# Who issues the weight loads of the first projections: ScalarE in place of SyncE

## The chip, the cores and the metric

The kernel runs on one core of a Trainium2 chip. The metric is the device time of one execution in microseconds (us). TensorE (PE) multiplies, VectorE (DVE), ScalarE (ACT) and GpSimd (POOL) work on tiles in SBUF, and SyncE (SP) only issues transfers. Each of SP, ACT and POOL has a DMA queue of its own; 16 DMA engines move the data of all of them. The engines run side by side and wait for each other on semaphores. An instruction that issues a transfer is held on its engine behind the waits that stand before it.

## The reference, cut to what matters

One step of a decoder layer over a prompt of 512 rows and 8 sequences of 8 new rows (64 "sample" rows), with D = 1024. The part that the change touches is the modulation and the combined input projection:

```
mod = (silu(c) @ w_ada + b_ada).reshape(B, 6, 1, D_MODEL)      # w_ada is 1024 x 6144
shift1, scale1, gate1, shift2, scale2, gate2 = [mod[:, i] for i in range(6)]
h = x * (1 + scale1) + shift1
proj = h @ w_in                                                # w_in is 1024 x 3072
qa, ka, va, qb, kb, vb = split(proj)                           # six sections of 512
qa, ka, qb, kb get rotary positions
...
oa, win_state = attend_a(qa, ka, va)     # windows over a cache of 2048 rows
ob = attend_b(qb, kb, vb)                # pages of a cache of 2048 rows
mixed = concat(oa, ob) @ w_o ; layer norm ; ConvFFN ; layer norm
```

Among the outputs are the updated window caches: for each of the 8 sequences 2040 rows of the old keys and 2040 of the old values, moved up by 8 rows, and the new rows behind them.

## The kernel before, in words

**Weights.** A weight is loaded in chunks of 1024 x 512 floats (2 MB) into slots of the tile `ring`. `CHUNKS` lists them; chunks 0 to 3 are the first four pieces of w_ada and chunks 4 to 9 the six sections of w_in (`("in", 0)` to `("in", 5)`). From chunk 4 on, two slots alternate (`SLOT_OF`), so section c can be loaded only when section c - 2 is used up. TensorE says so by the semaphore `w_used`, after the last unit of a section. The matmuls are done in parts of float32r: VectorE and GpSimd split a section into a high part and a rest (`split_in`, and the job "split" of GpSimd, L774), and each product is three matmuls (`product`, L1723 to L1725); for the sample rows two (`sample_product`, L1718 and L1719).

**Units.** `units` are the 30 pairs (section s, tile t), s from 0 to 5 and t from 0 to 4, where t = 4 (`TP`) is the sample tile. Unit n is section n // 5, tile n % 5. Sections 0, 1, 3 and 4 are queries and keys; their results go through VectorE's rotation (L1232 to L1236), GpSimd's addition (L788) and a transposition on TensorE (L1783). Sections 2 and 5 are values; ScalarE evicts them (L910). ScalarE also evicts the transposed queries (L916). The result of a unit lies in one of four PSUM banks, so TensorE waits for the eviction of unit n - 4 before unit n.

**The late modulation.** The other eight pieces of w_ada (4 to 11) are needed only after the attention, but their products are done here, in between. Piece ch is multiplied just before unit `LATE_UNIT[ch]` (L1666; units 3, 6, 10, 13, 16, 20, 23 and 26), and summed one unit later (L1679). All of them use one buffer, `late`, so piece ch + 1 can be loaded only when product ch is done (`ada_mm`).

**Copies.** `COPY_UNIT` puts eight copies of a window cache from DRAM to DRAM (4080 KB each, `move_window`, L586) at the units 1, 4, 8, 11, 14, 18, 21 and 24. The other eight come much later. Counted in the order of issue, they are called the first to the eighth copy.

**Order of the issues.** SyncE issues all of these. It walks over the 30 units in a written order. At each unit of keys or values it first waits for the result (`rope_ok` or `pj_a`) and stores it (L604, L608, L619, L622); at the last tile of a section it loads section s + 2 (`load_chunk(6 + s)`, L544), behind the wait for `w_used` (L542); at the units of `LATE_UNIT` it loads the next late piece (`load_late`, L582), behind the wait for `ada_mm` (L580); then comes the copy of this unit. At units of queries there is nothing to store and so no wait of that kind. ScalarE has in this stage a written list of jobs too, sorted by a number: the evictions "v" at n and "q" at n + 2.5. After the projections the attention over the caches begins, for which SyncE and GpSimd load 100 MB, and SyncE starts with it behind its last store.

Of the kernel before, what the change touches and what calls it, by code (L numbers as in the profile page):

```python
# [5 lines left out]
P = 128  # L6
# [10 lines left out]
TP = SEQ // P  # L17
# [11 lines left out]
CH = 512  # L29
# [14 lines left out]
SLOT_OF = [0, 1, 2, 3] + [0, 1] * 3 + [i % 2 for i in range(19)]  # L44
CHUNK_AT = {c: i for i, c in enumerate(CHUNKS)}
# [7 lines left out]
def chunk_before(n):  # L53

    return max((i for i in range(n) if SLOT_OF[i] == SLOT_OF[n]), default=None)
# [7 lines left out]
LATE_UNIT = {4: 3, 5: 6, 6: 10, 7: 13, 8: 16, 9: 20, 10: 23, 11: 26}  # L63
# [15 lines left out]
def build(nc, a, o, spill):  # L79
# [6 lines left out]
    with ctx:  # L86
# [3 lines left out]
        def sem(name):  # L90
            return ctx.enter_context(nc.semaphore(name))
# [4 lines left out]
        def bk(i):  # L96

            return wide[i // 2][:, 512 * (i % 2):512 * (i % 2) + 512]
# [37 lines left out]
        def slot(i, t=ring):  # L136
            return t[:, i * SLOT:(i + 1) * SLOT].rearrange("p (k n) -> p k n", k=KT_D)

        def part(t, at, n):
            return t[:, at:at + n]  # L140
# [19 lines left out]
        late = part(room, 12288, KT_D * CH).rearrange("p (k n) -> p k n", k=KT_D)  # L160
# [106 lines left out]
        w_in_slot = [sem(f"w_loaded_{i}") for i in range(N_SLOTS)]  # L267
        w_used = sem("w_used")
# [9 lines left out]
        ada_mm = sem("ada_product")  # L278
# [13 lines left out]
        late_in = sem("late_modulation_loaded")  # L292
# [103 lines left out]
        units = [(s, t) for s in range(6) for t in range(TP + 1)]  # L396
# [22 lines left out]
        for r, n in enumerate(rope_units):  # L419
            sec, t = units[n]  # L420
# [56 lines left out]
        def page_numbers(eng, b, g):  # L477

            at = N_PAGES * b + 4 * g
            _, numbers = nc.values_load_multi_w_load_instructions(pages[0:1, at:at + 4], engines=[eng.engine],  # L480
                                                                  min_val=0, max_val=a["cache_k"].shape[1] - 1)
            return numbers
# [36 lines left out]
                        .then_inc(landed, 16)  # L519


        @block.sync
        def _(sp):
            def load_chunk(n):
                kind, i = CHUNKS[n]
                if (prev := chunk_before(n)) is not None and CHUNKS[prev][0] == "down":
                    half, kg = divmod(CHUNKS[prev][1], 3)
                    sp.wait_ge(g_used, FT * half + min(FT, 8 * kg + 8))
                elif prev is not None:
                    sp.wait_ge(w_used, prev + 1)  # L530
                s = w_in_slot[SLOT_OF[n]]
                dst = slot(SLOT_OF[n])
                src = a[{"ada": "w_ada", "in": "w_in", "o": "w_o", "up": "w_up", "down": "w_down"}[kind]][0]
                src = src.rearrange("(k p) n -> p k n", p=P)
                if kind == "up":
                    for g in range(2):
                        sp.dma_start(dst[:, :, 256 * g:256 * g + 256],
                                     src[:, :, DFF * g + 256 * i:DFF * g + 256 * i + 256]).then_inc(s, 16)
                elif kind == "down":
                    half, kg = divmod(i, 3)  # L540
                    nk = min(8, FT - 8 * kg)
                    sp.dma_start(dst[:, 0:nk, :], src[:, 8 * kg:8 * kg + nk, CH * half:CH * half + CH]).then_inc(s, 16)  # L542
                else:
                    sp.dma_start(dst, src[:, :, CH * i:CH * i + CH]).then_inc(s, 16)  # L544
# [29 lines left out]
            sp.dma_start(pages[:, :], a["page_table"].rearrange("b n -> (b n)").rearrange("(o n) -> o n", o=1)).then_inc(page_in, 16)  # L574


            def load_late(ch):

                if ch > 4:
                    sp.wait_ge(ada_mm, ch)  # L580
                src = a["w_ada"][0].rearrange("(k p) n -> p k n", p=P)
                sp.dma_start(late, src[:, :, CH * ch:CH * ch + CH]).then_inc(late_in, 16)  # L582

            def move_window(i, names=(("cache_win_k", "wks"), ("cache_win_v", "wvs"))):
                for name, dst in names:
                    sp.dma_start(o[dst][0, i, 0:PAST - DS], a[name][0, i, DS:PAST]).then_inc(copied, 16)  # L586


            def flat(ap):
                return ap.rearrange("t h d -> t (h d)")  # L590

            load_late(4)
            n_rope = n_v = 0
            for n, (s, t) in enumerate(units):
                kb_rows = slice(P * t, P * t + P)
                if s in (0, 3):
                    n_rope += 1
                elif s in (1, 4):
                    m = s // 3
                    sp.wait_ge(rope_ok, n_rope + 1)  # L600
                    if t < TP:
                        st = n_rope % 4
                        dst = flat((o["wkp"] if m == 0 else o["kkp"])[0, 0])[kb_rows, :]
                        sp.dma_start(dst, stage[:, st, :]).then_inc(stg[st], 16)  # L604
                    else:
                        if m == 0:
                            for b in range(DB):
                                sp.dma_start(flat(o["wks"][0, b])[PAST - DS:PAST, :],  # L608
                                             k_s[DS * b:DS * b + DS, 0, :]).then_inc(out_sem, 16)
                        else:  # L610
                            sp.dma_start(o["kks"][0].rearrange("b s h d -> (b s) (h d)"), k_s[:, 1, :]).then_inc(out_sem, 16)
                    n_rope += 1
                else:
                    m = s // 3
                    n_v += 1
                    sp.wait_ge(pj_a, n_v)
                    if t < TP:
                        dst = flat((o["wvp"] if m == 0 else o["kvp"])[0, 0])[kb_rows, :]
                        sp.dma_start(dst, vp[:, t, m, :]).then_inc(out_sem, 16)  # L619
                    elif m == 0:  # L620
                        for b in range(DB):
                            sp.dma_start(flat(o["wvs"][0, b])[PAST - DS:PAST, :],  # L622
                                         v_s[DS * b:DS * b + DS, 0, :]).then_inc(out_sem, 16)
                    else:
                        sp.dma_start(o["kvs"][0].rearrange("b s h d -> (b s) (h d)"), v_s[:, 1, :]).then_inc(out_sem, 16)
                if t == TP:
                    if s < 4:
                        load_chunk(6 + s)
                for ch, at in LATE_UNIT.items():
                    if at == n and ch < 11:  # L630
                        load_late(ch + 1)
                if n in COPY_UNIT:
                    i, which = COPY_UNIT[n]
                    move_window(i, (("cache_win_k", "wks") if which == "k" else ("cache_win_v", "wvs"),))
# [222 lines left out]
        def _(act):  # L857
# [40 lines left out]
            jobs = []  # L898
            for n, (s, t) in enumerate(units):
                if n in v_units:  # L900
                    jobs.append((n, "v", n))
                if n in tr_units and s in (0, 3) and t < TP:
                    jobs.append((n + 2.5, "q", n))
            for _, what, n in sorted(jobs):
                s, t = units[n]
                rows = P if t < TP else NS
                if what == "v":
                    act.wait_ge(pj_mm, n + 1)
                    dst = vp[:, t, s // 3, :] if t < TP else v_s[:, s // 3, :]
                    nc.scalar.activation(dst, bk(n % 4)[0:rows, :], ACT.Copy).then_inc(pj_a, 1)  # L910
                else:
                    k = tr_units.index(n)
                    act.wait_ge(qk_t, k + 1)
                    src = bk(4 + k % 2).rearrange("p (f t) -> p f t", f=4)
                    m0 = 4 * (s // 3)
                    nc.scalar.activation(qt[:, m0:m0 + 4, P * t:P * t + P], src, ACT.Copy).then_inc(qk_a, 1)  # L916
# [167 lines left out]
        def _(dve):  # L1084
# [120 lines left out]
            jobs += [(n + 0.55, "late_sum", ch) for ch, n in LATE_UNIT.items()]  # L1205
            dve.wait_ge(rope_in, 16)
            for _, what, n in sorted(jobs):
                if what == "late_rows":
                    ada_rows(n)
# [1004 lines left out]
```

## Time and profile before

| what | us |
|---|---|
| median of 3 runs | 1175.63 (1174.1 to 1181.54) |
| the profiled execution, its own time | 1176.66 |
| its span in the profile | 1175.0 |
| TensorE busy | 1023.7 (87% of the span) |
| VectorE busy | 827.1 (70%) |
| GpSimd busy | 450.5 (38%) |
| ScalarE busy | 270.8 (23%) |
| queue of SyncE (and ScalarE) | 54.2% of 16 DMA engines |

Times in the rows are counted from the start of the span. A busy share is an average over stages with different limits, so for this change the stretch of the projections counts, from 58 to 269 us, and in it what TensorE waits for. TensorE's granted clock is shown as a share of full speed: 1.00 is 2.4 GHz, and 0.50 is 1.2 GHz.

### The profile page before, as it was taken

Reading aid. Unit: us, or ns where it says so; the run is one execution under the profiler, and the core shown is the slowest. Engines: PE = TensorE matmul, PEld = TensorE weight load, DVE = VectorE, ACT = ScalarE, POOL = GpSimd, SP = SyncE. Lnnn points to the kernel's source line nnn. Section 1 sums busy time; section 2 is a strip of 40 time slices with the busy share of each in tenths; the row PEclk is TensorE's granted clock in tenths of the full one; section 3 lists DMA queues with packets and bytes.
Section 4 is the critical chain, followed back from the end, with each engine's and each line's share of the span. In section 5 each row is a group of like instructions: output and inputs, shape, how many; then the busy total and the mean of one; then the engine's idle time right before and its main releaser. Section 6 shows DMA issues by size and latency. Waiting matters only on the chain.

```text
span 1175.0 us, 23900 instructions
## 1 busy us (share of the span) xinstructions
PE 1023.7 (87%) x9297; PEld 832.1 (71%) x9297; DVE 827.1 (70%) x1545; ACT 270.8 (23%) x600; POOL 450.5 (38%) x575
## 2 busy tenths in 40 slices
PE   4599989995788888888888969999999999998994
PEld 2377657673566666566676759999999999776873
DVE  1637545644886877888876784676676767999978
ACT  0300000001343433343352032323232323000001
POOL 0423223214243444434406034565566656333323
PEclk8699999998898989898998988999999999999998
DMA  8948799978899999999963151677676622414102
GB/s 299 410 157 312 269 351 365 318 246 266 289 365 368 327 337 368 349 331 331 337 253 127 42 190 47 219 255 277 248 253 250 215 73 75 155 60 147 53 2 80
DMA packets 101030, 276.54 MB, mean 235 GB/s; under 512 B 9608, under 2 KB 33174, under 8 KB 97317
## 3 DMA queue, kind: packets, MB, share of 16 engines
q1 hardware_dynamic: 85701, 223.56, 54.2%
q0 software_dynamic: 15168, 51.39, 12.6%
q8 instruction: 74, 1.21, 0.4%
q14 instruction: 39, 0.32, 0.1%
q10 hardware_dynamic: 48, 0.05, 0.0%
HBM read 264.60 MB, written 76.69 MB: 290 GB/s over the span
## 4 chain that ended last, share of the span: by engine, by line
PE 53%; DVE 16%; issue 15%; DMA 6%; POOL 5%; SPq 2%; POOLq 2%; ACT 1%; ACTq 0%; DVEq 0%; PEldq 0%
PE wide L1723 15%; PE wide L1724 14%; PE wide L1725 14%; DMA ring<-in_w_ada 2%; DVE ring_r L1180 2%; POOLq L480 1%; PE wide L1666 1%; POOL room L509 1%; DVE ht_r L1533 1%; DMA room<-in_w_ada 1%; DVE ring L1260 1%; POOL x_sb L509 1%; POOL x_sb L805 1%; PE wide L1807 1%; DVE ring_r L1179 1%
## 5 line engine op out<-in xcount | busy, mean ns | idle before, releaser
L828 POOL TENSOR_TENSOR ring_r<-ring,ring_r 128x1024 fp32r<-128x1024 f32 x70 | 180.8, 2592 | 232.3 <-DVE ring_r L1139 201.1
L1723 PE MATMUL wide<-x_sb_r,ring_r 128*128 128x288 f32 x704 | 211.1, 300 | 11.4 <-DVE ht_r L1162 8.4
L1724 PE MATMUL wide<-ht_r,ring_r 128*128 128x288 f32 x704 | 209.3, 297 | 0.0
L1725 PE MATMUL wide<-x_sb_r,ring_r 128*128 128x288 f32 x704 | 208.7, 297 | 0.0
L1723 PEld LDWEIGHTS wide<-x_sb_r,ring_r 128*128 128x128 f32 x704 | 133.4, 190 | 14.3 <-issue 14.3
L1260 DVE STREAM_TRANSPOSE ring<-ring 128x512 f32<-128x512 f32 x208 | 129.0, 677 | 12.0 <-DMA ring<-in_cache_k 10.3
L1725 PEld LDWEIGHTS wide<-x_sb_r,ring_r 128*128 128x128 f32 x704 | 134.2, 191 | 0.0
L1724 PEld LDWEIGHTS wide<-ht_r,ring_r 128*128 128x128 f32 x704 | 133.8, 190 | 0.0
L1723 PE MATMUL wide<-ring_r,x_sb_r 128*128 128x512 f32 (+1 forms) x208 | 87.0, 418 | 11.9 <-DVE ht_r L1162 8.7
L1725 PE MATMUL wide<-ring_r,ht_r 128*128 128x512 f32 x216 | 87.2, 404 | 0.0
L1724 PE MATMUL wide<-ring_r,x_sb_r 128*128 128x512 f32 (+1 forms) x208 | 83.7, 402 | 0.0
L1548 DVE SCALAR_TENSOR_TENSOR room<-room,vec_t 128x512 f32<-128x512 f32 x44 | 55.4, 1260 | 40.0 <-ACT room L1056 40.0
L1048 ACT ACTIVATE room<-wide,vec_t 128x576 f32<-128x576 f32 x44 | 32.8, 744 | 207.1 <-PE wide L1725 202.3
L1725 PE MATMUL wide<-ring_r,room_r 128*128 128x512 f32 x192 | 77.5, 404 | 0.0
L1550 DVE SCALAR_TENSOR_TENSOR room<-room,vec_t 128x512 f32<-128x512 f32 x44 | 73.5, 1671 | 1.6
L774 POOL TENSOR_TENSOR ring_r<-ring,ring_r 128x512 fp32r<-128x512 f32 x24 | 33.5, 1401 | 88.1 <-ACT ring_r L876 44.1
L1139 DVE CAST ring_r<-ring 128x1024 fp32r<-128x1024 f32 x62 | 41.9, 687 | 34.0 <-DMA ring<-in_w_up 32.1
L1807 PE MATMUL wide<-room 128*128 128x128 f32 x320 | 53.9, 303 | 12.0 <-ACT room L950 8.6
L1723 PEld LDWEIGHTS wide<-ring_r,x_sb_r 128*128 128x128 f32 (+1 forms) x208 | 39.9, 192 | 32.6 <-issue 16.7
L517 POOL DMA_DIRECT2D x_sb<-in_cache_v x60 | 33.0, 550 | 72.5 <-issue 71.4
L1723 PE MATMUL wide<-ring_r,ht_r 128*128 128x512 f32 x136 | 55.8, 410 | 5.0 <-DVE room L1574 2.9
L1807 PEld LDWEIGHTS wide<-room 128*128 128x128 f32 x320 | 44.1, 205 | 22.1 <-ACT room L950 12.8
(271 smaller groups left out, 2119.4 us busy)
## 6 DMA issues: line engine op xcount, KB each, us to landing
ring<-in_cache_k SPq DMA_DIRECT2D x128, 256.0 KB
out_wks<-in_cache_win_k SPq DMA_DIRECT2D x8, 4080.0 KB, 19.5
out_wvs<-in_cache_win_v SPq DMA_DIRECT2D x8, 4080.0 KB, 19.3
ring<-in_w_up SPq DMA_DIRECT2D x22, 1024.0 KB, 7.6
room<-in_w_ada SPq DMA_DIRECT2D x8, 2048.0 KB, 9.7
ring<-in_cache_win_k SPq DMA_DIRECT2D x16, 1024.0 KB
x_sb<-in_cache_v POOLq DMA_DIRECT2D x60, 256.0 KB, 5.4
room<-in_cache_v POOLq DMA_DIRECT2D x56, 256.0 KB, 5.3
```

Source lines behind the costliest of these rows:

```text
L517: eng.dma_start(home[t:P:4, :, :], flat_v[1][bass.ds(pg, 1)].rearrange("a (i m) h d -> m (a i) (h d)", i=4))\
L774: nc.gpsimd.tensor_tensor(rest, w, high.bitcast(F32), ALU.subtract).then_inc(win_pool, 1)
L828: nc.gpsimd.tensor_tensor(rest, w, high.bitcast(F32), ALU.subtract).then_inc(wl_rest, 1)
L1048: nc.scalar.activation(u_b[:, k % 2, 2:2 + NT].rearrange("p (h t) -> p h t", h=2), pair, ACT.Identity, bias=vec_t[:, 0, 48 + f:49 + f]).th ...
L1139: nc.vector.tensor_copy(pair_of(n, slice(k, k + 2))[0], slot(SLOT_OF[n])[:, k:k + 2, :]).then_inc(wl_high, 1)
L1260: last = nc.vector.transpose(ktg[:, G % NK, :, 32 * t:32 * t + 32], kraw[G % NK][:, t, :].rearrange("p (g d) -> p g d", d=32))
L1548: then(nc.vector.scalar_tensor_tensor(out=c_p, in0=u_b[:, k % 2, 1:1 + SEQ], scalar=tap(1), in1=c_p, op0=ALU.mult, op1=ALU.add))
L1550: nc.vector.scalar_tensor_tensor(out=c_p, in0=u_b[:, k % 2, 0:SEQ], scalar=tap(0), in1=c_p, op0=ALU.mult, op1=ALU.add)
L1723: nc.tensor.matmul(out, left[0], right[0], start=first, stop=False)
L1724: nc.tensor.matmul(out, left[0], right[1], start=False, stop=False)
L1725: return nc.tensor.matmul(out, left[1], right[0], start=False, stop=last)
L1807: last = nc.tensor.matmul(bank[:, 0:P], pt_b[:, u % 2, P * kb:P * kb + P], vp[:, kb, m, P * (n // 2):P * (n // 2) + P], start=(kb == 0), s ...
```

## The change

The seven loads of the late pieces 5 to 11 and the four loads of the sections 2 to 5 leave SyncE's list and come into ScalarE's list of jobs. A late load has the number of its unit plus 0.3, a section the number of the sample tile's unit plus 0.4, so that each stands behind the eviction of values of the same unit and ahead of the evictions with larger numbers. The waits before them are the same ones (`ada_mm` and `w_used`), now on ScalarE. The load of piece 4, the first sections and all stores and copies stay on SyncE.

```
+        def load_late(eng, ch):
+            if ch > 4:
+                eng.wait_ge(ada_mm, ch)
+            src = a["w_ada"][0].rearrange("(k p) n -> p k n", p=P)
+            eng.dma_start(late, src[:, :, CH * ch:CH * ch + CH]).then_inc(late_in, 16)
...
-            load_late(4)
+            load_late(sp, 4)
...
-                if t == TP:
-                    if s < 4:
-                        load_chunk(6 + s)
-                for ch, at in LATE_UNIT.items():
-                    if at == n and ch < 11:
-                        load_late(ch + 1)
                 if n in COPY_UNIT:
...
+            jobs += [(at + 0.3, "late", ch + 1) for ch, at in LATE_UNIT.items() if ch < 11]
+            jobs += [(n + 0.4, "w_in", 2 + s) for n, (s, t) in enumerate(units) if t == TP and s < 4]
+            src_in = a["w_in"][0].rearrange("(k p) n -> p k n", p=P)
             for _, what, n in sorted(jobs):
+                if what == "late":
+                    load_late(act, n)
+                    continue
+                if what == "w_in":
+                    c = CHUNK_AT[("in", n)]
+                    act.wait_ge(w_used, chunk_before(c) + 1)
+                    act.dma_start(slot(SLOT_OF[c]), src_in[:, :, CH * n:CH * n + CH]).then_inc(w_in_slot[SLOT_OF[c]], 16)
+                    continue
```

## Rows read from the trace of the kernel before

**Rows 1.** Stretches: from:to, length, busy us (count) of each engine, PEclk, DMA share, GB/s.

```profile
151.00:157.00 6.00, 6.00 (x29) 3.03 (x22) 0.69 (x1) 0.00 (x0) 0.00 (x0) 0.72 0.97 340
58.00:269.00 211.00, 197.80 (x946) 143.46 (x946) 109.98 (x190) 10.37 (x18) 53.66 (x40) 0.97 0.81 285
300.00:590.00 290.00, 246.64 (x4589) 179.87 (x4589) 232.12 (x660) 107.50 (x349) 113.86 (x234) 0.93 0.97 340
```

**Rows 2.** Waits of PE, 55 to 275: us in total, times, longest.

```profile
PE wide L1666 <- DMA room<-in_w_ada: 3.6, 1, 3.6
```

**Rows 3.** Chain of waits in order of time: start, us, what.

```profile
137.74 12.79 DMA room<-in_w_ada
...
222.56 1.83 PE wide L1666 x16
...
243.86 1.83 PE wide L1666 x16
```

**Rows 4.** Timeline of SP: start, us, what it issues.

```profile
23.38 5.25 SPq L544 DMA_DIRECT2D ring<-in_w_in  x1
...
48.48 4.21 SPq L586 DMA_DIRECT2D out_wks<-in_cache_win_k  x1
...
89.21 0.59 SPq L586 DMA_DIRECT2D out_wvs<-in_cache_win_v  x1
...
120.77 0.52 SPq L586 DMA_DIRECT2D out_wks<-in_cache_win_k  x1
...
136.67 0.41 SPq L544 DMA_DIRECT2D ring<-in_w_in  x1
...
142.54 0.52 SPq L586 DMA_DIRECT2D out_wvs<-in_cache_win_v  x1
...
169.99 0.58 SPq L586 DMA_DIRECT2D out_wks<-in_cache_win_k  x1
174.42 0.40 SPq L582 DMA_DIRECT2D room<-in_w_ada  x1
...
219.25 0.53 SPq L586 DMA_DIRECT2D out_wks<-in_cache_win_k  x1
```

**Rows 5.** Timeline of ACT, evictions of units 10 and 14: start, us, [idle before <- releaser].

```profile
130.96 0.60 ACT L910 ACTIVATE room<-wide 128x512 f32<-128x512 f32 x1 [33.08 <-PE wide L1725]
...
166.20 0.59 ACT L910 ACTIVATE ring<-wide 64x512 f32<-64x512 f32 x1 [5.77 <-PE wide L1725]
```

**Rows 6.** Timeline of PE: behind unit 9, product 7, product 9.

```profile
122.20 0.63 PE L1783 MATMUL wide<-ident,mix 128*128 128x128 f32 x4 [0.45 <-PE wide L1719]
...
150.58 3.18 PE L1666 MATMUL wide<-room,c_t 128*9 128x512 f32 x16 [3.65 <-DMA room<-in_w_ada]
...
197.48 1.90 PE L1666 MATMUL wide<-room,c_t 128*9 128x512 f32 x16
```

**Rows 7.** DMA issues of 130 to 145 and 172 to 180: count, KB, us to landing.

```profile
room<-in_w_ada SPq DMA_DIRECT2D x1, 2048.0 KB, 12.8
...
room<-in_w_ada SPq DMA_DIRECT2D x1, 2048.0 KB, 21.0
```

**Rows 8.** DMA packets of 122 to 134 (third copy) and 79 to 85 (a load).

```profile
DMA packets 69, 4.19 MB, mean 350 GB/s; under 512 B 4, under 2 KB 4, under 8 KB 4
...
DMA packets 1018, 2.06 MB, mean 344 GB/s; under 512 B 10, under 2 KB 10, under 8 KB 1018
```

**Rows 9.** DMA queues (q1 SP, q0 POOL), 341 to 346, then 346 to 351: packets, MB.

```profile
q1 hardware_dynamic: 193, 1.31, 65.0%
q0 software_dynamic: 184, 0.70, 35.0%
...
q0 software_dynamic: 216, 0.82, 52.1%
q1 hardware_dynamic: 262, 0.75, 51.1%
```

**Rows 10.** Timeline of POOL: last slice of the split of section 4.

```profile
202.35 1.41 POOL L774 TENSOR_TENSOR ring_r<-ring,ring_r 128x512 fp32r<-128x512 f32 x1 [0.97 <-DVE ring_r L1177]
```

More of the change, by code:

```diff
@@ L574, in _ @@
             sp.dma_start(pages[:, :], a["page_table"].rearrange("b n -> (b n)").rearrange("(o n) -> o n", o=1)).then_inc(page_in, 16)
[L577 to L582, printed above, removed]
             def move_window(i, names=(("cache_win_k", "wks"), ("cache_win_v", "wvs"))):
```

## The prediction

> **What bounds the kernel now.** I began with the stretches that the change touches. The thirty units of the first projections run from 58 to 269 us. There TensorE is busy for 197.80 of 211.00 us, and ScalarE for 10.37 [rows 1]. So TensorE sets the pace and leaves some 13 us, and ScalarE has room. Next I asked which of those gaps a load ends. The waits of TensorE name one, 3.6 us for a piece of the modulation's weights [rows 2]. The chain of waits shows where: the piece for product 7, issued at 137.74, is on the path for 12.79 us until the product starts [rows 3]. TensorE's own timeline puts the product at 150.58, after 3.65 us of idleness [rows 6], so the piece was wanted at 146.93. Afterwards TensorE runs slow: the granted clock is 0.72 from 151 to 157 [rows 1], which is 1.2 GHz for about 3.4 us of them, and with the time from 150.58 to 151 half of 3.8 us is lost, 1.9 us. This wait costs 3.65 + 1.9 = 5.6 us in all. After the projections the cache attention keeps the DMA engines at 0.97 [rows 1], so it takes as long as before, and what the projections gain or lose moves the end of the kernel one for one.
>
> **The moved instructions.** Eleven loads of 2 MB change queue: seven pieces (5 to 11) and four sections of w_in (2 to 5). SyncE's issues of them take about 0.4 us each [rows 4]. Eleven of those on a ScalarE that is idle for 200 of 211 us are hidden between its evictions; I cost them at nothing, and at 11 x 0.4 = 4.4 us if all fell on the path. Only a full queue would make them longer: SyncE's early issue of a section took 5.25 us with several loads ahead of it [rows 4], and ScalarE has at most two loads waiting at almost every issue. The waits that move with the loads are for products that TensorE finishes before the next eviction is due, so no eviction stands behind a late one.
>
> **When loads are issued.** Section 3 is free after unit 9, at about 122 us [rows 6]; SyncE reached it only at 136.67, behind the stores of unit 9 [rows 4]. ScalarE issues it at once: 14 us earlier. Piece 7 goes out behind ScalarE's eviction of unit 10 (130.96 plus 0.6 [rows 5]), at 131.6 in place of 137.74. Section 4 follows the eviction of unit 14 (166.20 + 0.6 [rows 5]), at 166.8; before it went out just ahead of the fifth copy. Piece 9 stays at 174.42, since its product 8 sets it. SyncE loses the blocks in front of its copies of the window caches too: the second copy goes out right after the first at 48.48, not at 89.21 [rows 4]. The DMA engines have the room, with a share of 0.81 over the projections [rows 1], and only piece 5 is wanted near it; this is free. The third (120.77), fourth (142.54) and fifth (169.99) are set by row stores and stay where they are, the fifth some 0.4 us earlier.
>
> **How loads and copies share.** Everything on SyncE's queue went in order, so a load waited for the copies ahead of it and no more. Now they stand in two queues. A copy of 4.18 MB is some 64 packets: 69 packets, 4 of them small, carry 4.19 MB in the stretch that holds the third copy, 65 KB each. A load is 2 KB a packet (1018 for 2.06 MB) [rows 8]. With 16 engines a copy is four packets on each. All 64 start after 122, 1.3 us behind the issue, and before 134; at some 3 us for a packet (16 x 65 KB at 350 GB/s) a copy takes 13.7 us. A load is 64 packets an engine, done in less than the stretch's 6 us; I take 5.3. What a load gets beside a copy is not shown by the trace. Bound it: by equal bytes it gets half; by one packet in turn it gets 2 KB against 65 KB, so it stands still until the copy has ended. The nearest rows are two queues in the attention stage. From 341 to 346 us they moved 193 and 184 packets, but 1.31 and 0.70 MB: equal packets, not equal bytes. From 346 to 351 it is 262 and 216 packets and 0.75 and 0.82 MB: nearer to equal bytes, but the engines were less full there [rows 9]. I go by the first, the fuller stretch, and take turns by the packet.
>
> The Trainium skill, "DMA: Bandwidth & Descriptors", section "Queues, rings and completion order", also has each DMA engine go round its queues at packet boundaries, but counts some 9 to 17 descriptors as one packet; no row here shows groups. If it is so, the sum is plus 3 us in place of the one below (second rival).
>
> **The sum, taking turns by the packet.** *Piece 7.* The third copy's data run from about 122 to 135.8 (issue + 1.3 us, four packets). Section 3 hardly moves until then and ends at 141; piece 7 follows. At 142.54 + 1.3 = 143.8 the fourth copy starts, with some 2.8 us of piece 7 left. It stands still for the copy's 13.7 us and lands at 160.5. Before, both came ahead of that copy, in order, and piece 7 landed after 12.8 us, at 150.5 [rows 7]. Product 7 is 9.9 us later. Its slow clock stays as it is.
>
> *Section 4 and piece 9* (in the times of before, to which the 9.9 us are added). Section 4 starts at 168.1; the fifth and sixth copies arrive from 170.9, both at once, since SyncE has no wait between units 15 and 18. About 2.5 us of it are left, and the two copies take 27 us, until 198. Section 4 lands at about 199.5 less what it got in eight turns (0.7 us), so near 198.5, and piece 9 5.3 us later, at 203.7. Before, section 4 was ahead of both copies, and piece 9 between them, landing 21.0 us after 174.42 at 195.4 [rows 7], in time for its product at 197.48 [rows 6]. Now that product starts at 203.7, 6.2 us late, and runs at the slow clock (3.18 us, as product 7 [rows 6], against 1.90), and unit 20 behind it loses another 1.1 us. The split of section 4 starts up to 5 us late as well; its last slice by GpSimd came at 202.35 [rows 10] and then comes near 208, inside unit 20, which is hidden by the wait for piece 9; without that cover it alone would cost those 5 us. Sum of this place: 6.2 + 1.3 + 1.1 = 8.6 us.
>
> *The rest.* Piece 11 now leaves at 224.4, behind product 10 [rows 3], inside the seventh copy (219.25 [rows 4]), which ends at about 234; it lands by 240, and its product is at 243.86 [rows 3]. Pieces 5, 6, 8 and 10 and sections 2 and 5 have 5 us of slack or more, or no copy beside them. These cost nothing; if one of the covers is missing, it costs at most the 5.3 us of a load.
>
> Total: 9.9 + 8.6 = 18.5 us. The profiled execution took 1176.66 us, so 1195.2; it is 1.0 us above the median of 1175.63, so I forecast **1194**. By turns of up to four load packets the result is within 3 us of it; errors of 2 us in a copy's start move each term by 2. The case's own range is 1185 to 1201.
>
> **Rivals.**
> *Shares by bytes.* Then section 3 (from 123.5) is done by 134 beside the third copy, and piece 7 by about 144, before 146.93. The wait of 5.6 us goes, and section 4 and piece 9 are both done by 193. 1176.66 - 5.6 = 1171; the late stores of SyncE no longer delay anything. For it: the second stretch of [rows 9], and that the same engines have work from either queue at any time. Against it: the first stretch. It decides from a share of about a third: below that, piece 7 is not home at 146.93.
>
> *Turns of some 16 load packets.* The load gets 1.3 us after each packet of a copy. Section 3 ends at 140.5, piece 7 with two turns of the fourth copy in it at 152.7, 2.1 us later than before; piece 9, four turns behind section 4, lands at 200 and costs 1. Plus 3: 1179, range 1174 to 1183. It is the Trainium skill's rule above, worked out with the durations of this trace. "Issuing engines are not separate DMA queues", on the same page of the Trainium skill, says as well that issuing from several engines saves only the sequencer's time; no row here shows it, and by it alone nothing would change.
>
> *Only one collision.* The fourth copy or the pair misses its load by a microsecond or two, because stores or evictions fall otherwise than I took them. Then one of 9.9 and 8.6 is left: 1185 to 1187, just within 1%.
>
> *It doesn't do what it says.* ScalarE's queue, with two loads of 2 MB standing still in it, could hold ScalarE at its third issue (section 5, near 197), as SyncE was held for 5.25 us [rows 4]. The evictions of queries behind it come late while TensorE waits for piece 9 anyway; at most 3 us more.
>
> **Chances.** By the packet with both collisions 0.45; by bytes 0.29; groups of packets 0.13; one collision 0.08, near the limit, so a third of it slower; blocked ScalarE on top 0.01, slower; something outside this list that gains over 1% 0.04. A measurement of this kernel can't tell less than about 1% from no change, so within 1% is 1164 to 1187. Slower 0.49, same 0.47, faster 0.04. The range of 8 in 10 reaches from the case by bytes, 1170, to the upper end of the likeliest, 1200.
>
> **What would show it.** In the profile after: the wait of the ada product for its piece (L1666) grows from one of 3.6 us to one near 13 and one near 6, at 147 and some 10 us past 197; landings of section 3, piece 7, section 4 and piece 9 near 19, 29, 32 and 29 us after issue, counted in that order; the second copy starts before 60 us; the attention stage is as long as before. By bytes, those landings are 10 to 20 us, and no such wait is left. If the waits are there but the attention stage is shorter, then the stage was not bound by its transfers, and my one for one is wrong.

## The result, and the profile after

The changed kernel takes 1193.16 us in the median of 4 runs (1192.59 to 1193.81), against 1177.89 for the kernel before in 4 runs of its own (1174.1 to 1181.54). The ratio is **1.0153, interval 1.0123 to 1.0182**: slower by one and a half per cent. The two medians by themselves are 15.3 us apart, a ratio of 1.0130, which lies inside the interval. The forecast was 1194.

The first two groups of before have these answers in the stretches and in the waits of TensorE after the change:

```profile
58.00:269.00 211.00, 182.18 (x868) 130.57 (x867) 109.50 (x190) 8.37 (x14) 53.53 (x40) 0.92 0.75 266
151.00:162.00 11.00, 0.00 (x0) 0.00 (x0) 0.00 (x0) 0.00 (x0) 0.00 (x0) 0.61 0.83 308
```

```profile
PE wide L1671 <- DMA room<-in_w_ada: 21.3, 2, 13.6
```

Against [rows 1], TensorE is busy 15.6 us less in the same stretch, and for 11 us from 151 on it does nothing at all while the DMA engines are busy for 83%. Against [rows 2], one wait of 3.6 us has become two, 21.3 us together. TensorE's timeline places them (product 6, product 7, product 9, product 10; L1671 is L1666 of before):

```profile
124.35 1.90 PE L1671 MATMUL wide<-room,c_t 128*9 128x512 f32 x16
...
162.14 3.60 PE L1671 MATMUL wide<-room,c_t 128*9 128x512 f32 x16 [13.60 <-DMA room<-in_w_ada]
...
217.51 3.60 PE L1671 MATMUL wide<-room,c_t 128*9 128x512 f32 x16 [7.66 <-DMA room<-in_w_ada]
...
240.34 1.90 PE L1671 MATMUL wide<-room,c_t 128*9 128x512 f32 x16
```

The issues of ScalarE and SyncE after the change, to be held against [rows 4]:

```profile
123.62 0.38 ACTq L908 DMA_DIRECT2D ring<-in_w_in  x1
...
132.56 0.38 ACTq L527 DMA_DIRECT2D room<-in_w_ada  x1
...
178.72 0.37 ACTq L908 DMA_DIRECT2D ring<-in_w_in  x1
...
186.70 0.37 ACTq L527 DMA_DIRECT2D room<-in_w_ada  x1
```

```profile
52.29 0.59 SPq L586 DMA_DIRECT2D out_wvs<-in_cache_win_v  x1
...
122.36 0.52 SPq L586 DMA_DIRECT2D out_wks<-in_cache_win_k  x1
...
144.15 0.52 SPq L586 DMA_DIRECT2D out_wvs<-in_cache_win_v  x1
...
182.14 0.52 SPq L586 DMA_DIRECT2D out_wks<-in_cache_win_k  x1
182.70 0.59 SPq L586 DMA_DIRECT2D out_wvs<-in_cache_win_v  x1
...
287.87 1.02 SPq L643 DMA_DIRECT2D ring<-in_cache_win_k  x2
```

Each issue of ScalarE takes 0.4 us and comes when the working had it: section 3 some 13 us and piece 7 some 5 us earlier than before. Section 3 leaves earlier and arrives no earlier (at 144.3 us, against 136.67 + 7.9 = 144.6 before), and piece 7 leaves earlier and arrives 11.5 us later. The four loads of ScalarE's rows above, in the same order, with the time from issue to landing:

```profile
ring<-in_w_in ACTq DMA_DIRECT2D x1, 2048.0 KB, 20.7
...
room<-in_w_ada ACTq DMA_DIRECT2D x1, 2048.0 KB, 29.5
...
ring<-in_w_in ACTq DMA_DIRECT2D x1, 2048.0 KB, 33.6
...
room<-in_w_ada ACTq DMA_DIRECT2D x1, 2048.0 KB, 30.8
```

Before, pieces 7 and 9 took 12.8 and 21.0 us [rows 7]. What happens meanwhile is in the DMA queues (packets, MB, share) from 186 to 209 us, while the fifth and the sixth copy run on SyncE's queue, q1, and section 4 and piece 9 stand in ScalarE's, q10:

```profile
DMA packets 263, 8.09 MB, mean 352 GB/s; under 512 B 23, under 2 KB 23, under 8 KB 142
## 3 DMA queue, kind: packets, MB, share of 16 engines
q1 hardware_dynamic: 136, 7.83, 97.0%
q10 hardware_dynamic: 126, 0.24, 3.8%
```

136 packets on one queue, 126 on the other; 7.83 MB against 0.24 MB. The engines are full, and the loads get a thirtieth of the bytes.

**A better yardstick than the total.** What comes after the projections took between 900 and 912 us in the executions of this study, with no tie to the variant that I can see, and the first 120 us differ by some 3 us. So for each profiled execution I also give the time from product 6 to the moment when SyncE issues its first cache load. For before this is 147.26 us, from these rows; for after 287.87 - 124.35 = 163.52, which is 16.3 us more.

```profile
122.76 1.90 PE L1666 MATMUL wide<-room,c_t 128*9 128x512 f32 x16
```

```profile
270.02 1.02 SPq L649 DMA_DIRECT2D ring<-in_cache_win_k  x2
```

| kernel | median us | ratio to before, interval | product 6 to first cache load, less 147.26 |
|---|---|---|---|
| after | 1193.16 | 1.0153 (1.0123 to 1.0182) | +16.3 |
| e1 after, copies in 2 KB packets | 1170.45 | 0.9946 (0.9923 to 0.9969) | -3.6 |
| e2 before, copies in 2 KB packets | 1176.49 | 0.9993 (0.9973 to 1.0013) | -0.1 |
| e3 only the sections moved | 1172.42 | 0.9953 (0.9932 to 0.9974) | -3.7 |
| e4 only the pieces moved | 1184.44 | 1.0071 (1.0047 to 1.0095) | +8.7 |
| e5 after, copies in 8 KB packets | 1190.38 | 1.0133 (1.0090 to 1.0176) | +13.0 |
| e6 after, four copies gated | 1175.27 | 1.0010 (0.9982 to 1.0039) | -2.0 |
| e7 after, fourth copy gated | 1184.02 | 1.0054 (1.0024 to 1.0085) | +6.1 |
| e8 after, no copies | 1168.93 | 0.9944 (0.9917 to 0.9971) | -7.0 |
| e9 after, piece 7 ahead of section 3 | 1181.28 | 1.0029 (1.0003 to 1.0055) | +4.7 |
| e10 as e9, copies at other units | 1176.29 | 0.9989 (0.9959 to 1.0018) | +0.2 |

Ratios are to runs of the kernel before on the same chip. The last column is from one execution each, and it has a noise of its own. In every kernel TensorE stands for 1.9 us ahead of the sums of product 6, between 129 and 135 us, and then runs at 1.2 GHz for a while. From 124 to 145 us the granted clock is 0.84 in e2, e3, e4 and e9, and 0.92 in before and in all others: here are before and e3.

```profile
124.00:145.00 21.00, 18.77 (x85) 14.62 (x78) 10.41 (x16) 1.20 (x2) 4.54 (x4) 0.92 0.83 279
```

```profile
124.00:145.00 21.00, 18.78 (x73) 14.93 (x73) 9.62 (x16) 1.20 (x2) 4.06 (x3) 0.84 0.99 351
```

The 0.08 of 21 us make 1.7 us, so without them these four would stand at -1.8, -5.4, +7.0 and +3.0. Why the slow stretch was longer in them isn't shown.

### The profile page after: what moved, and what is told of

Same layout as the page of the kernel before. It is cut to its first block, busy times and chain, and to the rows that moved or that the text cites. A ratio compares the mean times of both kernels' runs of the same rounds, so it can differ in the third digit from the quotient of the medians.

```text
span 1191.7 us, 23900 instructions
## 1 busy us (share of the span) xinstructions
PE 1022.1 (86%) x9297; PEld 830.3 (70%) x9297; DVE 823.1 (69%) x1545; ACT 270.8 (23%) x600; POOL 450.4 (38%) x575
## 4 chain that ended last, share of the span: by engine, by line
PE 47%; DVE 19%; issue 15%; DMA 9%; POOL 5%; POOLq 2%; SPq 1%; ACT 1%; ACTq 0%; DVEq 0%; PEldq 0%
PE wide L1728 13%; PE wide L1730 13%; PE wide L1729 13%; DMA room<-in_w_ada 5%; DMA ring<-in_w_ada 2%; DVE ht_r L1538 2%; PE wide L1671 2%; DVE ring_r L1185 2%; POOLq L480 1%; DVE ht_r L1539 1%; DVE room_r L1540 1%; POOL room L509 1%; PE wide L1868 1%; DVE x_sb L1613 1%; DVE ring_r L1144 1%
## 5 line engine op out<-in xcount | busy, mean ns | idle before, releaser
L1729 PE MATMUL wide<-ht_r,ring_r 128*128 128x288 f32 x704 | 208.9, 297 | 0.0
L1265 DVE STREAM_TRANSPOSE ring<-ring 128x512 f32<-128x512 f32 x208 | 129.0, 678 | 14.9 <-DMA ring<-in_cache_k 14.4
L1868 PE MATMUL wide<-ring,x_sb 128*32 128x128 f32 (+1 forms) x1792 | 58.8, 276 | 2.8 <-DVE ring L1265 2.7
```

What stands on the lines that cost most here:

```text
L1265: last = nc.vector.transpose(ktg[:, G % NK, :, 32 * t:32 * t + 32], kraw[G % NK][:, t, :].rearrange("p (g d) -> p g d", d=32))
L1729: nc.tensor.matmul(out, left[0], right[1], start=False, stop=False)
L1868: last = nc.tensor.matmul(bank[32 * nn:32 * nn + 32, at:at + nk], qbd[:, w % 2, g].rearrange("p i q -> p (i q)"), keys[:, g, 0:nk], start= ...
```

## The experiments

**Is it the size of the packets?** e1 changes nothing in the changed kernel but the form of the eight copies; e2 does the same to the kernel before.

```
-  sp.dma_start(o[dst][0, i, 0:PAST - DS], a[name][0, i, DS:PAST])
+  turned = lambda ap: ap.rearrange("(a b r) h d -> b a (r h d)", b=16, r=1)
+  sp.dma_start(turned(o[dst][0, i, 0:2032]), turned(a[name][0, i, DS:DS + 2032]))
+  sp.dma_start(o[dst][0, i, 2032:PAST - DS], a[name][0, i, DS + 2032:PAST])
```

> The changed kernel, but the eight window copies of the projections are written as 16 strands of 127 single rows (2 KB a packet in place of 65 KB) and a small rest. Theory 'turns' (a DMA engine serves the two queues one packet each in turn): a load now gets about half of the engines beside a copy; section 3 is in by 136, piece 7 by about 146, and both waits of the ada products (13.6 and 7.7 us in the changed kernel) shrink to under 2 us; time near 1171 to 1175, unless copies in small packets are slow themselves or hold SyncE at the issue. Rival 'queue order' (SyncE's queue goes first, whatever its packets): the waits stay near 13 and 8 us, time 1190 to 1194. Rival 'memory' (loads are slow beside any copy from DRAM to DRAM): waits stay too.

1170.45 us. The wait of 13.6 us is down to 1.7, and the one of 7.7 is gone; section 3 and piece 7 landed at 139.9 and 148.7 us, 3 to 4 us later than I had them. The rivals "queue order" and "memory" are out: the same copies stand in the same queue and move the same bytes, and only the packets are smaller. One thing more differs: SyncE is held 4 to 13 us at the issue of each small rest, so the sixth copy leaves 10 us behind the fifth and not right behind it. The third and the fourth, which make the first collision, keep their times (120.86 and 142.66).

> The kernel before with the same copies in packets of 2 KB; all loads and copies stay on SyncE's queue, in order. All theories: a load waits for the copies ahead of it as before, so nothing changes but the copies' own speed: 1174 to 1182, the wait for piece 7 still 3 to 5 us. If SyncE is held at the issue of a copy with 2032 packets, its later loads go out later, and the wait for piece 7 grows.

1176.49 us, ratio 0.9993: on one queue the size of the packets is worth nothing. The wait for piece 7 is 1.9 us, where 3 to 5 were forecast. The gain of e1 is therefore not in faster copies.

**Packets of 8 KB.** e5 is e1 with r = 4 and 1920 rows.

> The changed kernel with the eight copies in packets of 8 KB (16 strands of 30 packets, and a small rest). 'Turns, one packet each': a turn is about 0.32 us for the copy and 0.08 for the load, so some 30 of a load's 64 packets on an engine pass beside one copy. Section 3 is in near 140, piece 7 has some 16 packets left when the fourth copy comes and lands near 150.5: a wait of 3 to 4 us in place of 13.6. Piece 9 lands near its product, a wait of 0 to 1 us in place of 7.7. Time 1176 to 1178. Rival 'groups of packets' (several load packets a turn): no waits, 1171. Rival 'large and small only' (the cost hangs on something else of the strands): like the 2 KB run, 1170, or like the changed kernel, 1193.

1190.38 us, where 1176 to 1178 was forecast: the size was missed by 12 us, the law was not. The waits for pieces 7 and 9 were 11.85 and 6.91 us, in place of 3 to 4 and 0 to 1. Here are the two queues from 128 to 136 us, with a copy on q1 and a load on q10, in three kernels: after, e5 and e1.

```profile
q1 hardware_dynamic: 32, 2.09, 82.3%
q10 hardware_dynamic: 32, 0.07, 2.8%
```

```profile
q1 hardware_dynamic: 270, 2.21, 74.4%
q10 hardware_dynamic: 264, 0.54, 23.9%
```

```profile
q10 hardware_dynamic: 731, 1.50, 53.6%
q1 hardware_dynamic: 734, 1.50, 49.4%
```

Packets are one to one at 65 KB, 8 KB and 2 KB alike (32 : 32, 270 : 264, 734 : 731), and the load's share of the bytes is 3%, 20% and 50%. I had put that into numbers as if the 16 engines ran evenly. They don't. Of e5, from 152 to 158 us:

```profile
q1 hardware_dynamic: 256, 2.10, 100.0%
q10 hardware_dynamic: 37, 0.05, 2.8%
```

By turns on all engines there would be as many load packets as copy packets. There are 37 for 256, and 11 of the 37 are writes under 512 B; 16 such writes come with every load, which I take for the engines reporting their parts done. From 154 to 158 us next to nothing of the load is left:

```profile
q1 hardware_dynamic: 163, 1.34, 100.7%
q10 hardware_dynamic: 8, 0.02, 1.7%
```

Eight load packets in 4 us are one each 0.5 us, beside 163 of the copy on 16 engines, 10 for each. That fits one engine that still takes turns, while the others are done, and of the product's 11.85 us of waiting the last 5 or so were for that one. A load has landed when its last engine is done, so even a copy with a load share of 20% delays the tail of a load by most of the copy. That a slow engine is so because of the small row stores ahead is my guess; the trace doesn't name engines.

**Each part alone.** In e3 the list of ScalarE has only the jobs "w_in", and SyncE keeps the late pieces:

```
-            jobs += [(at + 0.3, "late", ch + 1) for ch, at in LATE_UNIT.items() if ch < 11]
...
+                for ch, at in LATE_UNIT.items():
+                    if at == n and ch < 11:
+                        load_late(sp, ch + 1)
```

> One part of the change alone: ScalarE issues the four sections of w_in, the late pieces stay on SyncE. 'Turns': section 3 stands still beside the third copy and ends beside piece 7 by 147; piece 7 is ahead of the fourth copy on the same queue, so its wait is under 1 us; section 4 stands still beside the fifth copy, until about 185, and is in by 188, before its split at 193.65; piece 9 goes between the fifth and sixth copy as before. No wait left: 1176.7 - 5.6 = 1171. Rival (the loss comes from section loads that start inside copies): section 4 late, 1180 or more.

1172.42 us, with no wait for a piece left. Section 3 landed 20.8 us after its issue and section 4 after 23.3 (7.9 and 8.0 before), so both did stand still beside a copy, and it cost nothing, because the splits that use them come 15 and 4 us after the landings. This version beats the kernel before by half a per cent. By the yardstick it gains 3.7 us and not the forecast 5.6; the longer slow stretch behind product 6 makes up 1.7 of the difference.

e4 is the opposite: the jobs "late" on ScalarE, `load_chunk(6 + s)` back on SyncE.

> The other part alone: ScalarE issues the late pieces 5 to 11, the sections stay on SyncE. 'Turns': piece 7 leaves at 131.6, stands still until the third copy's end at 136, then shares with section 3 and is in by about 146: no wait there, minus 5.6 us. Piece 9 leaves at 174.4 with the fifth and sixth copy in SyncE's queue, one behind the other without it, and lands only behind both, near 209 in the times of before: 12 us late and 2.4 us of slow clock. Sum 1176.7 - 5.6 + 14.4 = 1185. Rival (the sections' move makes the loss): 1171.

1184.44 us, and 8.7 us by the yardstick, where the sum had -5.6 + 14.4 = 8.8. That fit is luck: from product 6 to product 8 it gained 3.7 us, and behind product 8 it lost 12.4, each some 2 us off (1.7 of the first is the slow stretch behind product 6). Piece 9 landed 37.9 us after its issue; TensorE at product 9:

```profile
208.57 3.57 PE L1673 MATMUL wide<-room,c_t 128*9 128x512 f32 x16 [14.84 <-DMA room<-in_w_ada]
```

Here nothing but its own load stands in ScalarE's queue, and it still waits for both copies. That is the second collision by itself. Piece 7 stood only beside the rest of the third copy, landed 11.9 us after its issue and made no wait. So for the first collision both parts together are needed: section 3 ahead of piece 7 on one queue, behind the third copy, pushes it into the fourth.

**Taking copies out of the way.** e6 and e7 hold copies of the changed kernel back; e8 leaves the eight copies out, so these parts of its outputs are never written.

```
                     i, which = COPY_UNIT[n]
+                    if n in (11, 18, 21):                      # e7: if n == 11
+                        sp.wait_ge(late_in, 16 * {11: 4, 18: 6, 21: 7}[n])
+                    elif n == 14:                              # e6 only
+                        c = CHUNK_AT[("in", 4)]
+                        sp.wait_ge(w_in_slot[SLOT_OF[c]], slot_count(c))
```

> The changed kernel with one wait alone: the fourth copy waits for the landing of piece 7. This takes the first collision away and leaves the second. 'Turns': piece 7 lands near 146, so its wait of 13.6 us goes; piece 9 still lands behind two copies, 6 to 9 us late and with 2.4 us of slow clock. 1193.2 less (13.6 + 1.9 to 2.4) = 1177 to 1178. If the two waits were one effect passed on, this would come out at 1171 or at 1193.

1184.02 us, some 60% of the loss gone (+6.1 in place of +16.3). The first wait is down to 2.1 us while the second is still 5.3, so the two collisions are separate, as stated. But I forecast 1177 to 1178 and missed what the held copy hits next: it leaves at 149.10 and is in the way of piece 8, which had been free. Its product waits 4.25 us and runs slow:

```profile
173.69 3.60 PE L1673 MATMUL wide<-room,c_t 128*9 128x512 f32 x16 [4.25 <-DMA room<-in_w_ada]
```

> The changed kernel, but four of SyncE's copies wait until the load they would hit has landed: the fourth for piece 7, the fifth for section 4, the sixth for piece 9, the seventh for piece 10. Copies keep their 65 KB packets. 'Turns': piece 7 lands near 146, section 4 near 174, piece 9 near 193, no wait at any ada product; 1171, as good as the run with 2 KB packets. Rival (two queues are slower in themselves): some of the 13.6 and 7.7 us stays.

1175.27 us with a range of 1170.70 to 1185.43; by the yardstick -2.0. The big waits are gone, but four of 0.2 to 2.2 us are left (4.7 us in all). The largest is piece 7's own: with no copy beside its end it landed 18.2 us after its issue, at 149.1, and not near 146. The other three (1.55, 0.17 and 0.72 us) are for pieces 8, 10 and 11, which the held copies now delay. No gain over the kernel before is shown.

> The changed kernel with the eight copies of the projections left out (these parts of the window outputs are not written). 'Turns': no load stands beside a copy, no wait at any ada product; 1170 to 1172. The attention stage keeps its length, since no copy ran into it. If it came out well below 1170, the copies would cost more than these waits, for example in the attention stage or in the stores.

1168.93 us, 1 us under the range of the forecast, and -7.0 by the yardstick. No product waits for a piece: with no copies at all, two queues make no such wait. I take it as the floor; e1 and e3 are within 4 us of it. Of the 7.0 us, 1.6 lie between product 9 and product 10 (23.37 us here, 25.01 before), where no slow stretch follows TensorE's stop.

**Order within ScalarE's queue, and places of the copies.**

```
-  jobs += [(n + 0.4, "w_in", 2 + s) for ...
+  jobs += [(n + (0.4 if s != 1 else 1.35), "w_in", 2 + s) for ...
   e10 also:
+  COPY_UNIT = {1: ..., 4: ..., 5: ..., 8: ..., 11: ..., 14: ..., 21: ..., 24: ...}
```

> The changed kernel with one order changed on ScalarE: section 3 is loaded behind piece 7, in place of ahead of it. 'Turns': piece 7 runs from the third copy's end at 136 to about 142, before the fourth copy's first packet at 144; its wait of 13.6 us goes. Section 3 then stands still beside the fourth copy and lands near 160, just in time for its split at about 161. The second collision stays: piece 9 some 6 to 9 us late. Time 1178 to 1181. If section 3 is late too, some us more. Rival (the first wait is the price of the copy as such, whatever stands in the queue): 1193.

1181.28 us, +4.7. Piece 7 landed 12.1 us after its issue in place of 29.5, and its wait is gone, with the same copies at the same units. The number 1.35 puts the load of section 3 just behind that of piece 7. Section 3 was not caught by the fourth copy, as I had expected, but landed at 148.7 us; what is left of the loss is the second collision, a wait of 10.1 us for piece 9. So the first wait of the changed kernel was no price of the copy as such; it was a piece that missed the gap between two copies. How little it missed it by shows in the changed kernel from 148.5 to 162 us, the time of the fourth copy and of the row stores behind it: q10 moved 126 packets there, writes under 512 B among them, so at most an eighth of the 1024 of piece 7 were open when the copy came.

```profile
q1 hardware_dynamic: 244, 4.33, 83.9%
q10 hardware_dynamic: 126, 0.24, 4.7%
```

> As the run with piece 7 first, and four copies leave two units later or earlier so that no two stand behind one another beside a wanted load: the copies go out at the units 1, 4, 5, 8, 11, 14, 21 and 24 (before: 1, 4, 8, 11, 14, 18, 21, 24). 'Turns': the third runs from 102 to 116 beside piece 6, which lands near 120 against a need at 123; the sixth at 170 holds section 4 until 184, and piece 9 lands near 192, before 197.5. No wait left but for a us or two: 1171 to 1173, as the run with 2 KB packets, with copies of 65 KB. It tells whether the law is good enough to place copies by.

1176.29 us, where 1171 to 1173 was forecast; no gain is shown. (Its profiled execution, of 1184.51 us, is the slowest of its 12, with 912 us behind the projections.) No product waits for a piece any more, as planned. But the copy of unit 11 came at 142.79, 1.2 us earlier than the one at 144.01 in e9, and caught section 3 before its end: it landed 30.5 us after its issue, not 17.5, and the split waited 6.4 us for it, and TensorE 5.4 us for the slices. The law held and a plan by it isn't robust. Which load is caught hangs on a microsecond.

## Why the prediction was right, step by step

*TensorE sets the pace in the projections, and the rest passes one for one.* Right. The stage of the cache attention kept its length, as far as one execution each can tell where all lie between 900 and 912: 1175.0 - 270.02 = 905.0 us of the span are left at the first cache load before, and 1191.7 - 287.87 = 903.8 after. The DMA engines are at 0.99 in it, against 0.97 [rows 1]:

```profile
310.00:600.00 290.00, 236.67 (x4442) 173.22 (x4444) 230.63 (x654) 107.11 (x351) 112.20 (x231) 0.92 0.99 342
```

*The issues cost nothing on ScalarE.* Right, eleven of 0.4 us between evictions. ScalarE was held at an issue only in e9 and e10, where two loads were issued one right behind the other.

*The choice between bytes and packets.* Right, and now shown: one to one at three sizes. The rival "shares by bytes" and the rival "turns of some 16 load packets" are out. This kernel of before had only one fair hint, the stretch of equal packets in [rows 9]; the second stretch there spoke the other way, and I can't say why.

The rule of the Trainium skill, "DMA: Bandwidth & Descriptors", section "Queues, rings and completion order", that an engine goes round its queues at packet boundaries, agrees with the traces. The 9 to 17 descriptors that it counts to a packet do not: the turn of a load was a single record of 2 KB, by the counts above.

*The first collision, 9.9 us.* From product 6 to product 7 it was 150.58 - 122.76 = 27.82 us before and 162.14 - 124.35 = 37.79 after: 9.97 us. The collision is as told, but that it fits to a tenth is luck, for the steps inside it were off by more. I had the fourth copy start 1.3 us behind its issue. It was issued at 144.15, and from 144 to 148 us the queues moved this:

```profile
DMA packets 804, 1.63 MB, mean 408 GB/s; under 512 B 7, under 2 KB 7, under 8 KB 804
q10 hardware_dynamic: 735, 1.50, 96.7%
q1 hardware_dynamic: 69, 0.13, 8.6%
```

All 804 packets are under 8 KB, so no packet of the copy is among them; the 69 of SyncE's queue are row stores that were issued ahead of it. So the copy came 2.5 us or more later than in the working, and it found at most an eighth of piece 7 left, not half. The two errors cancel: from the copy's start to the landing of piece 7, at 162.06, it took 14 us at most, where I had 16.7 (143.8 to 160.5). At the rate of the rows above, 126 packets are 0.7 us of load. By this estimate a copy that came 0.7 us later would have met nothing, which is the rival "only one collision".

*The second, 8.6 us.* Mis-sized, with errors of opposite sign. From product 7 to product 9 it is 46.90 us before (197.48 - 150.58 [rows 6]) and 55.37 after, so product 9 came 8.5 us later, not 6.2. Most of this is a slip in my sum: 198 + 2.5 - 0.7 is 199.8 for section 4 and not 198.5, so by its own terms piece 9 lands at 205.1 and its product is 7.6 us late. Another 0.7 us is the slow clock of product 7, which I had left as it was: the product took 3.60 us in place of 3.18, and product 8 came 22.59 us behind it in place of 21.87 (172.45 - 150.58). The landings were all 1 to 2 us later than I had written (20.7, 29.5, 33.6 and 30.8 us against 19, 29, 32 and 29). And again the copy, issued at 182.14, started later than 1.3 us behind its issue: from 180.2 to 185.5 us 880 packets passed on q10, nearly all of them section 4's, and none of 65 KB on q1, whose 114 packets carried 0.12 MB.

```profile
184.73 1.90 PE L1671 MATMUL wide<-room,c_t 128*9 128x512 f32 x16
```

```profile
q10 hardware_dynamic: 880, 1.80, 93.3%
q1 hardware_dynamic: 114, 0.12, 6.3%
```

So about a seventh of section 4 was left when the two copies came, not half; it landed at 212.3 all the same, behind both, since its last engine counts.

But from product 9 to product 10 it was 25.01 us before, and 22.83 after: 2.2 us come back. Before, TensorE stood 1.9 us in that place, ahead of the sums of product 9. The trace names no releaser, but VectorE's copy of the rows of product 9 (L1125), which had its turn behind slices of the split of section 4, ended at 207.73, just ahead of them. Then TensorE ran at 0.53 of full clock from 208.9 to 212.4. After, the split began at 212.32, was well under way by the time piece 9 let TensorE go on, and neither the stop nor a slow stretch behind it is left; only product 9 itself runs slow.

```profile
207.83 1.03 PE L1679 MATMUL wide<-sum,mix 128*128 128x9 f32 x8 [1.93 <-issue]
...
222.49 1.91 PE L1666 MATMUL wide<-room,c_t 128*9 128x512 f32 x16
```

```profile
212.32 0.43 DVE L1182 CAST ring_r<-ring 128x512 fp32r<-128x512 f32 x1 [6.30 <-DMA ring<-in_w_in]
```

8.47 - 2.18 = 6.29, and 9.97 + 6.29 = 16.26, the whole of the measured 16.3. So the forecast of 18.5 us was too large by some 2 us in the projections. That the total still fits to a microsecond is partly luck, for two reasons. The profiled execution was 1.6 us later than before already at product 6, ahead of anything the change could delay. And the kernel before has its median at 1177.89 in the four runs of the result, where the forecast was added to 1175.63: the medians differ by 15.3 us, and I had forecast 18.4.

*The rest at nothing.* Right for pieces 5, 6, 8, 10 and 11: none of their products waits. One remark beside the sum did not hold: the prediction has it that less than about 1% can't be told from no change, but the intervals of the runs here are 0.2 to 0.4% each way.

## What to carry to other kernels

Before a load is moved to a second queue, look at the packet sizes on the first. The DMA engines alternate by the packet, so a load in 2 KB packets beside a copy in 65 KB packets gets 3% of the bytes, while behind the same copy in one queue it loses only the copy's rest; give the bulk transfer packets as small as the load's (8 KB still cost 1.3%), or leave urgent loads in its queue, ahead of it, and move only those with slack. Cost a load by its last engine and not by the mean, and don't lay plans on gaps of a microsecond.

## What the runs showed that I had not expected

- Copies from DRAM to DRAM in single rows of 2 KB are as fast as in 65 KB: the third copy, alone in its queue, landed 15.4 us after its issue before and 15.2 us in e2. In e1 from 130 to 140 us both queues together moved 4.04 MB, at full engines:

```profile
DMA packets 1990, 4.04 MB, mean 404 GB/s; under 512 B 16, under 2 KB 16, under 8 KB 1990
q1 hardware_dynamic: 995, 2.04, 52.8%
q10 hardware_dynamic: 995, 2.01, 51.9%
```

- ScalarE was held 4.76 us at an issue in e9, with one load of 2 MB issued 0.4 us before it (4.87 in e10, at the same place). How much a queue takes isn't shown by it: before, SyncE issued two such loads 1.07 us apart (136.67 [rows 4] and 137.74), and neither was held:

```profile
130.82 0.37 ACTq L527 DMA_DIRECT2D room<-in_w_ada  x1
131.24 4.76 ACTq L908 DMA_DIRECT2D ring<-in_w_in  x1
```

```profile
137.74 0.43 SPq L582 DMA_DIRECT2D room<-in_w_ada  x1
```

- The length of a wait alone doesn't tell whether TensorE goes on at 1.2 GHz. After 2.24 us in e6 the product took 1.90 us, at full speed; after 1.93 us in e2 it took 3.52 us.
